# A hybrid encoder layer: the first norm applied behind the up projection, six accumulators through up and down, and waits moved in the first round, the first SSD group, the last norms and the tail

## The chip, the cores and the metric

The kernel runs on one core of one Trainium2 chip, as one launch. The metric is the device time of the launch in microseconds. Names of engines: TensorE (PE in the rows, PEld its weight loads), VectorE (DVE), ScalarE (ACT), GpSimd (POOL), and SyncE (SP), whose queue issues the weight loads.

## What is computed

One inference step of one layer, for 256 prompt frames and 32 sample frames together (T = 288 columns), all in fp32:

```python
proj = x @ w_in                                  # gates | z | xBC | dt | q_a | kv_a
y_ssm = SSD(causal_conv(xBC), dt) ... @ w_ssm_proj   # 8 groups of 4 heads, grouped RMSNorm
y_mla = attention(latent q, latent kv) @ w_mla_proj  # 16 heads, in 4 rounds of 4
mix = (sigmoid(g_ssm) * y_ssm + sigmoid(g_mla) * y_mla) @ w_out
h = LN1(ALPHA * x + mix)                         # over 1024 features, gain ln1_g, offset ln1_b
y = LN2(ALPHA * h + relu(h @ w_up)**2 @ w_down)  # w_up 1024 x 4096, w_down 4096 x 1024
```

Further outputs are the new latents, the rotated keys, the SSD states and the last conv rows.

## The kernel before

**Layout.** Features lie on the partitions, frames on the columns. Every dense weight comes in chunks of 128 x 1024 floats (512 KB), 204 loads in the order of `chunk_order()`: q and kv latents, four conv blocks (x0 to x3), four attention rounds with seven conv blocks each, eight SSD groups with two z blocks, two gate blocks and two chunks of the MLA projection (m), the SSM projection (s), the output projection (8 chunks, o), the up projection (32, u), the down projection (32, d).

**Splits.** A chunk passes a ring of five slots. SP loads it when the slot is free, ScalarE writes its high part (`hi`, L868), VectorE the rest (`lo`, L1242), and TensorE multiplies in three passes (`passes`, L406 to L408: high x high, high x low, low x high), 24 matmuls of 288 columns per chunk. On ScalarE and VectorE `ahead(name)` splits the chunk three places behind the named one, so the order of `ahead` calls among the other work is each engine's programme, written out by hand. Engines run in order: a wait blocks what stands behind it.

**Accumulators.** Dense results go to two banks of ps_acc in turns (`open_turn` waits for the evacuation of the block two turns earlier); four banks (ps_row, ps_cb, ps_tr, together ps_att) hold attention, SSD and the first half of s; ps_s and ps_ss hold sums and small products.

**Start and round 0.** GpSimd begins with four loads of the rotated key cache, kall. Later it copies conv edges (`conv`, L1764 and L1766), builds kab and kall from krot (L1777, L1779), then loads side, the latent caches and side_v. ScalarE evacuates each conv block (`conv_in`), VectorE adds three taps (`conv`, L1291), ScalarE applies silu (`conv_out_block`, L938). TensorE takes transposes of dt, acum and wend (L467) before dense x3.

**First SSD group.** VectorE and ScalarE finish conv block 31 before `decay_log(0)` (L1462 to L1472) and the exponentials. TensorE's `tokens(g, t)` (L676) waits for seg_sub and for btok (tr_free). In group 0 ScalarE and VectorE also split o (`o_high`, `o_low`, four calls of 1152 columns each).

**Last norms.** `spread(j, bank)` (L730) broadcasts a group's inverse deviation, `normed` (L1537) multiplies by it, and `norm_high` and `norm_low` split the result. Spreads 6 and 7 stand behind chunk s(0,0).

**First norm.** VectorE adds ax (ALPHA x) and each output block into d1 (`block_sum`, L1666), from block 4 on less a provisional mean. GpSimd adds blocks and squares (L1864), TensorE sums over the partitions with the ones matrix (`first_sum` L812, `last_sums` L816 to L821), VectorE makes mean and variance, ScalarE the root, VectorE the reciprocal (L1690), GpSimd subtracts the mean from six blocks (L1899). Then for each block: scale on VectorE (L1696), add the offset into h_h on ScalarE (L1198), h_l on VectorE (L1700). The first two up chunks wait for each h_lo.

**Up and down.** For an up block ScalarE takes the relu out of PSUM (L1209), VectorE squares (L1730), ScalarE writes ff_h, VectorE ff_l (L1722). Down sums 32 matmul groups per output block; the second norm goes as the first, and its output leaves in four transfers.

## Time and profile before

| | |
|---|---|
| median of 3 runs | 882.57 us (881.86 to 884.1) |
| profiled execution | 882.47 us |
| its span, first to last instruction | 880.7 us |
| mean granted TensorE clock | 0.987 |
| busy in the span | PE 95%, VectorE 62%, ScalarE 51%, GpSimd 11% |
| moved by DMA | 123.57 MB, 140 GB/s on average |

A row of waits names the waiting instruction, what released it, and the time in total, the number of times and the longest. A timeline row gives start, duration and instruction; a pause before it and its releaser stand in brackets; several instructions in a row are one entry with xcount. A group of instructions gives count, busy time, mean ns, and the idle time before them. A TensorE matmul's listed duration is modelled and overlaps its neighbours; the distance from start to start is what it costs. In a window row the busy times stand in the order PE, PEld, DVE, ACT, POOL.

### The profile page before, as it was taken

To read this page: it belongs to the slowest core of one execution; us is meant where nothing else is said; L and a number is where in the kernel's file an instruction comes from. 1 tells how busy PE (TensorE), PEld (TensorE's weight loads), DVE (VectorE), ACT (ScalarE), POOL (GpSimd) and SP (SyncE) were. 2 spreads that over 40 slices of the span, in tenths; PEclk is the share of its full clock that TensorE was granted. 3 is DMA by queue.
4 is the path that set the end of the run, shared out by engine and by line. 5 is a ranking of instruction groups with operands and counts; after the bars stand their busy time and mean duration, and the time that the engine had idled before them with its cause. 6 is when DMAs were issued, how large, how long until landed. Compare 5 with 4: busy or idle time off the path is not lost.

```text
span 880.7 us, 15552 instructions
## 1 busy us (share of the span) xinstructions
PE 833.2 (95%) x6363; PEld 789.3 (90%) x6363; DVE 550.2 (62%) x899; ACT 447.2 (51%) x745; POOL 95.1 (11%) x163
## 2 busy tenths in 40 slices
PE   5989999999999998899999999999859999999994
PEld 5978999999899998789999999899859999999994
DVE  4786646646646655877677677666477666644454
ACT  4684655555556557553555544453336555533332
POOL 1052010011101011000000000000160000000033
PEclk9999999999999999999999999999999999999997
DMA  8457335325325224344344334555423555555441
GB/s 305 124 167 266 97 98 168 120 95 169 102 91 174 88 70 142 102 130 135 125 133 131 126 128 120 186 167 168 134 82 125 167 165 167 167 168 168 145 143 54
DMA packets 34183, 123.57 MB, mean 140 GB/s; under 512 B 4224, under 2 KB 4368, under 8 KB 33856
## 3 DMA queue, kind: packets, MB, share of 16 engines
q1 hardware_dynamic: 30816, 110.67, 39.6%
q0 software_dynamic: 3104, 11.24, 3.7%
q8 instruction: 51, 0.84, 0.4%
q10 hardware_dynamic: 192, 0.66, 0.2%
q14 instruction: 20, 0.16, 0.1%
HBM read 118.52 MB, written 4.04 MB: 139 GB/s over the span
## 4 chain that ended last, share of the span: by engine, by line
PE 76%; DVE 8%; ACT 6%; DMA 4%; issue 3%; POOL 2%; SPq 0%; ACTq 0%; DVEq 0%; POOLq 0%
PE ps_acc L406 19%; PE ps_acc L408 19%; PE ps_acc L407 18%; DMA wraw<-in_wst 3%; PE ps_s L590 3%; ACT whi L868 2%; ACT prob L987 2%; DMA side_v<-in_ukT 1%; DVE wlo L1242 1%; PE ps_acc L503 1%; PE ps_row L704 1%; DVE prob L1403 1%; PE ps_ss L602 1%; PE ps_acc L505 1%; PE ps_acc L504 1%
## 5 line engine op out<-in xcount | busy, mean ns | idle before, releaser
L1242 DVE TENSOR_TENSOR wlo<-wraw,whi 128x1024 fp32r<-128x1024 f32 x204 | 250.4, 1229 | 214.9 <-ACT whi L868 214.1
L868 ACT CAST whi<-wraw 128x1024 fp32r<-128x1024 f32 x204 | 213.3, 1046 | 124.5 <-DMA wraw<-in_wst 124.2
L406 PE MATMUL ps_acc<-xh,whi 128*128 128x288 f32 x576 | 178.4, 310 | 9.3 <-DVE wlo L1242 8.6
L408 PE MATMUL ps_acc<-xh,wlo 128*128 128x288 f32 x576 | 170.9, 297 | 0.0
L407 PE MATMUL ps_acc<-xl,whi 128*128 128x288 f32 x576 | 169.0, 293 | 0.0
L406 PEld LDWEIGHTS ps_acc<-xh,whi 128*128 128x128 f32 x576 | 108.9, 189 | 16.6 <-DVE wlo L1242 8.9
L407 PEld LDWEIGHTS ps_acc<-xl,whi 128*128 128x128 f32 x576 | 109.9, 191 | 0.6
L408 PEld LDWEIGHTS ps_acc<-xh,wlo 128*128 128x128 f32 x576 | 108.7, 189 | 0.0
L406 PE MATMUL ps_acc<-h_h,whi 128*128 128x288 f32 x256 | 76.7, 299 | 6.4 <-DVE h_l L1700 6.3
L408 PE MATMUL ps_acc<-h_h,wlo 128*128 128x288 f32 x256 | 76.6, 299 | 0.0
L408 PE MATMUL ps_acc<-ff_h,wlo 128*128 128x288 f32 x256 | 75.9, 296 | 0.0
L406 PE MATMUL ps_acc<-ff_h,whi 128*128 128x288 f32 x256 | 75.9, 296 | 0.0
L407 PE MATMUL ps_acc<-h_l,whi 128*128 128x288 f32 x256 | 75.4, 295 | 0.0
L407 PE MATMUL ps_acc<-ff_l,whi 128*128 128x288 f32 x256 | 74.6, 292 | 0.0
L1291 DVE SCALAR_TENSOR_TENSOR cv<-xp,vec,cv 128x292 f32<-128x292 f32 x96 | 50.4, 525 | 10.8 <-ACT cv L933 8.3
L406 PEld LDWEIGHTS ps_acc<-h_h,whi 128*128 128x128 f32 x256 | 48.9, 191 | 7.1 <-issue 6.7
L407 PEld LDWEIGHTS ps_acc<-h_l,whi 128*128 128x128 f32 x256 | 49.5, 193 | 0.0
L407 PEld LDWEIGHTS ps_acc<-ff_l,whi 128*128 128x128 f32 x256 | 48.8, 191 | 0.1
L408 PEld LDWEIGHTS ps_acc<-h_h,wlo 128*128 128x128 f32 x256 | 48.7, 190 | 0.0
L406 PEld LDWEIGHTS ps_acc<-ff_h,whi 128*128 128x128 f32 x256 | 48.1, 188 | 0.1
L408 PEld LDWEIGHTS ps_acc<-ff_h,wlo 128*128 128x128 f32 x256 | 48.0, 187 | 0.0
L1766 POOL COPY cnew<-xp 128x6 f32<-128x6 f32 x32 | 14.8, 462 | 241.3 <-ACT xp L930 241.3
(356 smaller groups left out, 1818.9 us busy)
## 6 DMA issues: line engine op xcount, KB each, us to landing
wraw<-in_wst SPq DMA_DIRECT2D x204, 512.0 KB, 3.5
side<-in_ukT POOLq DMA_DIRECT2D x8, 256.0 KB, 3.8
side_v<-in_ukT POOLq DMA_DIRECT2D x8, 256.0 KB, 3.1
out_ssm<-s_out POOLq DMA_DIRECT2D x8, 256.0 KB, 2.5
x<-in_xT SPq DMA_DIRECT2D x2, 576.0 KB, 6.0
ax<-in_xT POOLq DMA_DIRECT2D x1, 1152.0 KB, 6.6
out_y<-d SPq DMA_DIRECT2D x4, 288.0 KB, 2.1
ckvT<-in_cacheT POOLq DMA_DIRECT2D x1, 1024.0 KB, 7.7
```

The costliest lines, as they stand in the source:

```text
L406: pe.matmul(out, w, mh, start=first, stop=False)
L407: pe.matmul(out, w, ml, start=False, stop=False)
L408: return pe.matmul(out, wl, mh, start=False, stop=last)
L503: pe.matmul(acc, ckv_h[:, k, f], hi, start=k == 0, stop=False)
L504: pe.matmul(acc, ckv_h[:, k, f], lo, start=False, stop=False)
L505: mm = pe.matmul(acc, ckv_l[:, k, f], hi, start=False, stop=k == RB - 1)
L590: mm = pe.matmul(ps_s[:, c * P:(c + 1) * P], ckvK[0:n, j, c * P:(c + 1) * P], ssT[0:n, j, :], start=j == 0, stop=j == 4)
L868: act.copy(whi[:, s % RING, :], wraw[:, s % RING, :]).then_inc(split_hi, 1)
L987: e = act.activation(prob[:, h4, a:b], prob[:, h4, a:b], ACT.Exp, bias=stat[:, 1, 4 * q + h4:4 * q + h4 + 1], accum_out=stat[:, 2, 4 * q + ...
L1242: tt(wlo[:, s % RING, :], wraw[:, s % RING, :], whi[:, s % RING, :].bitcast(F32), ALU.subtract).then_inc(split_lo, 1)
L1291: stt(cv[:, u, :], xp[:, u, 1 + tap:1 + tap + CW], v1(V_CONVW + tap * CB + b), cv[:, u, :], ALU.mult, ALU.add).then_inc(tap_chain if tap < ...
L1766: pool.tensor_copy(cnew[:, b, :].rearrange("p (a c) -> p a c", a=2), xp[:, u, 8:XW].rearrange("p (a c) -> p a c", c=36)[:, 6:8, 33:36]).th ...
```

## The change

**First norm.** The sum over x of the 8 blocks is made in round 0 (three adds on VectorE, one sum over ones on TensorE), and ScalarE makes cm = -ALPHA/1024 of it in round 1. ax becomes ALPHA x + cm, on VectorE (before: ALPHA x on ScalarE). For each output block, d1 is evacuated, ScalarE writes e_h = gamma d1 and the square, VectorE e_l. The up projection multiplies e, extended by two columns (gamma and the offset), so 290 columns instead of 288. Mean and inverse deviation come from reductions on VectorE and two sums over ones behind up(2). They are applied to the product: VectorE adds -mean times the gamma column and multiplies by the inverse deviation, ScalarE adds the offset column in the relu, squares, and casts. h itself is made in the down stage (`residual`).

**Accumulators.** Up and down use six banks in turn. `behind(b)` sets how far the evacuation lags: three to one blocks.

**Second norm.** The provisional mean is block 0's alone (first_sum behind d(1,1)); the running sums on TensorE stand ahead of d(7,3); squares are taken block by block; VectorE subtracts the mean from blocks 0 to 3 (before 0 and 1), GpSimd from 4 to 7 (before 2 to 7).

**Moves.** The kall loads go behind the kab copies on GpSimd, side_v's ahead of the cache loads; dense x3 ahead of the transposes; silu of block 2 behind the evacuation of qab; conv 31 behind decay_log(0); the o splits of VectorE into group 1 (ScalarE's into groups 0 and 1); norm_rows(0) behind start_state(4); spreads 6 and 7 behind s(1,0); norm_high(4) and normed(4), normed(5) ahead of a weight split; mix_low(6), mixed(7) and mix_low(7) ahead of one.

The diff, cut:

```diff
+UB = 6
+
+
+def behind(b):
+
+    return max(0, b - 3 + (b >= 12) + (b >= 20))
+
+
...
     dense(("x", 1), open_turn(("x", 1)))
     dense(("x", 2), open_turn(("x", 2)))
+    dense(("x", 3), open_turn(("x", 3)))
     pe.wait_ge(m_act, 6)
...
-    dense(("x", 3), open_turn(("x", 3)))
...
         pe.wait_ge(qnat_cp, i + 1)
         if i:
             pe.wait_ge(os_evac, i)
+            pe.wait_ge(cm_done, 1)
...
+        if i == 0:
+            pe.wait_ge(cm_red, 3)
+            pe.wait_ge(os_evac, 1)
+            pe.matmul(ps_ss[:, 0:T], ones, cm[:], start=True, stop=True).then_inc(cm_pe, 1)
...
         dense(("s", b, 0), ps_att[b], yn_rows, 0, True, False)
-        if b == 0:
+        if b == 1:
...
+    def first_sum():
+
+        pe.wait_ge(d_evac, 1)
+        pe.matmul(ps_s[:, 0:T], ones, d2[:, 0, :], start=True, stop=True).then_inc(ln_pe, 1)
+
+    def run_sums():
+
+        pe.wait_ge(ln_run, 10)
+        pe.matmul(ps_s[:, 0:T], ones, lnt[:, 1, 1, :], start=True, stop=False)
+        pe.wait_ge(ln_run, 11)
+        pe.matmul(ps_ss[:, 0:T], ones, lnt[:, 1, 2, :], start=True, stop=False)
+
+    def last_sums():
+        pe.wait_ge(d_evac, 8)
+        pe.matmul(ps_s[:, 0:T], ones, d2[:, 7, :], start=False, stop=True).then_inc(ln_pe, 1)
+        pe.wait_ge(ln_sq, 8)
+        pe.matmul(ps_ss[:, 0:T], ones, sq2[:, 7, :], start=False, stop=True).then_inc(ln_pe, 1)
...
-        if b == 4:
-            first_sum(0)
-    last_sums(0, d1)
...
+    def up(b):
+
+
         wait_split(("u", b))
-    out = [open_turn(("u", b)) for b in range(2)]
-    for k in range(KB):
-        pe.wait_ge(h_lo, k + 1)
-        for b in range(2):
-            mm = passes(out[b][:, 0:T], *part(("u", b), k), h_h[:, k, :], h_l[:, k, :], k == 0, k == 7)
-            if k == 7:
-                mm.then_inc(chunk_used, 1)
-    for b in range(2, FB):
-        dense(("u", b), open_turn(("u", b)), lambda k: (h_h[:, k, :], h_l[:, k, :]))
...
+        if b >= UB:
+            pe.wait_ge(u_evac, b - UB + 1)
+        elif b >= 4:
+            wait_evac(pe, ("o", 6))
+            wait_evac(pe, ("o", 7))
+        out = up_banks[b % UB]
+        for k in range(KB):
+            if b == 0:
+                pe.wait_ge(e_lo, k + 1)
+            mm = passes(out[:, 0:E], *part(("u", b), k), e_h[:, k, :], e_l[:, k, :], k == 0, k == 7)
+        mm.then_inc(chunk_used, 1)
+
+    pe.wait_ge(gb_lo, 2)
+    for b in range(FB):
+        up(b)
+        if b == 2:
+            for j, bank in enumerate((ps_s, ps_ss)):
+                pe.wait_ge(ln1_red, 3 * j + 3)
+                pe.matmul(bank[:, 0:T], ones, lnt[:, 0, 1 + j, :], start=True, stop=True).then_inc(ln1_pe, 1)
...
-        out = open_turn(("d", b, 0))
+        pe.wait_ge(u_evac, min(FB, FB + b - UB + 1))
+        if b >= UB:
+            pe.wait_ge(d_evac, b - UB + 1)
         for k in range(4):
-            dense(("d", b, k), out, ff_rows, 8 * k, k == 0, k == 3)
-            if b == 4 and k == 0:
-                first_sum(1)
-    last_sums(1, d2)
+            if b == KB - 1 and k == 3:
+                run_sums()
+            dense(("d", b, k), down_banks[b], ff_rows, 8 * k, k == 0, k == 3)
+            if b == 1 and k == 1:
+                first_sum()
+    last_sums()
...
-    conv_out_block(2)
...
         q_copy(i, 2, qab, 0)
+        if i == 0:
+            conv_out_block(2)
...
+        if i == 1:
+            act.wait_ge(cm_pe, 1)
+            act.activation(cm[:], ps_ss[:, 0:T], ACT.Identity, scale=-ALPHA / D_MODEL).then_inc(cm_done, 1)
...
+        act.wait_ge(cm_red, 3)
...
-    conv_out_block(CB - 1)
     wait_used(act, att_last)
-    act.wait_ge(conv_done, CB)
...
+        if g == 0:
+            conv_out_block(CB - 1)
...
+        if g == 1:
             o_high(2)
...
+        if g < 2:
+            o_high(3 * g)
...
+        if g == 0:
+            o_high(1)
...
+    mix_high(KB - 1)
     ahead(("o", 0))
-    mix_high(KB - 1)
...
+    def sum_square(b):
+        act.activation(sq1[:, b, :], d1[:, b, :], ACT.Square).then_inc(ln1_sq, 1)
+
+    def e_high(b):
+        wait_evac(act, ("o", b))
+        act.activation(e_h[:, b, 0:T], d1[:, b, :], ACT.Identity, scale=v1(V_LN1G + b)).then_inc(e_hi, 1)
...
+            act.copy(e_h[:, :, T:T + 1], v1(V_LN1G, KB).unsqueeze(2)).then_inc(gb_hi, 1)
+            act.copy(e_h[:, :, T + 1:E], v1(V_LN1B, KB).unsqueeze(2)).then_inc(gb_hi, 1)
+        if b >= 2:
+            e_high(b - 2)
+            sum_square(b - 2)
+    for b in range(KB - 2, KB):
+        e_high(b)
+        sum_square(b)
...
+    def activate(b):
+
+        act.wait_ge(u_step, 2 * b + 2)
+        act.copy(wb[:, b % 2:b % 2 + 1], up_banks[b % UB][:, T + 1:E]).then_inc(u_evac, 1)
+        act.wait_ge(u_evac, b + 1)
+        act.activation(rl[:, b % 2, :], rl[:, b % 2, :], ACT.Relu, bias=wb[:, b % 2:b % 2 + 1]
+                       ).then_inc(ff_step, 1)
+        act.wait_ge(ff_step, 2 * b + 1)
+        if b >= 2:
+            act.wait_ge(ff_lo, b - 1)
+        act.activation(ff[:, b % 2, :], rl[:, b % 2, :], ACT.Square).then_inc(ff_step, 1)
+        act.wait_ge(ff_step, 2 * b + 2)
         act.copy(ff_h[:, b, :], ff[:, b % 2, :]).then_inc(ff_hi, 1)
...
+        if b == 3:
+            act.wait_ge(ln1_step, 3)
+            act.activation(lnt[:, 0, 4, :], lnt[:, 0, 4, :], ACT.Sqrt, bias=v1(V_LNEPS)).then_inc(ln1_std, 1)
+        for u in range(behind(b - 1), behind(b)):
+            activate(u)
...
+        if i == 0:
+            dve.wait_ge(misc_done, 1)
+            tt(x0[:, 0:4, :], x0[:, 0:4, :], x0[:, 4:8, :], ALU.add).then_inc(cm_red, 1)
...
+    wait_used(dve, att_last)
+    decay_log(0)
     conv(CB - 1)
-    wait_used(dve, att_last)
-    dve.wait_ge(silu_done, CB)
-    decay_log(0)
...
+        if g == 1:
+            o_low(0)
...
+        if g == 1:
+            o_low(1)
...
+        if g == 1:
+            o_low(2)
+        elif g == 4:
+            norm_rows(0)
...
+    dve.wait_ge(ax_in, 16)
+    dve.wait_ge(cm_done, 1)
+    stt(ax[:], ax[:], ALPHA, cm[:].unsqueeze(1).to_broadcast([P, KB, T]), ALU.mult, ALU.add).then_inc(ax_done, 1)
...
+    mix_low(KB - 2)
+    mixed(KB - 1)
+    mix_low(KB - 1)
     ahead(("o", 0))
-    mixed(KB - 1)
-    mix_low(KB - 2)
-    mix_low(KB - 1)
...
+    def out_sum(b):
+        wait_used(dve, ("o", b))
+        tt(d1[:, b, :], ax[:, b, :], acc_of(("o", b))[:, 0:T], ALU.add).then_inc(acc_sem(("o", b)), 1)
+
+    def e_low(b):
+        dve.wait_ge(e_hi, b + 1)
+        stt(e_l[:, b, 0:T], d1[:, b, :], v1(V_LN1G + b), e_h[:, b, 0:T].bitcast(F32), ALU.mult,
+            ALU.subtract).then_inc(e_lo, 1)
...
+        out_sum(b - 1)
+        if b >= 2:
+            e_low(b - 2)
+    out_sum(KB - 1)
+    e_low(KB - 2)
+    e_low(KB - 1)
...
+    def scaled(b):
+
+        wait_used(dve, ("u", b))
+        if b >= 2:
+            dve.wait_ge(ff_step, 2 * b - 2)
+        acc = up_banks[b % UB]
+        stt(ff_t[:, b % 2, :], lnt[:, 0, 3, :], acc[:, T:T + 1], acc[:, 0:T], ALU.mult, ALU.add
+            ).then_inc(u_step, 1)
+        dve.wait_ge(u_step, 2 * b + 1)
+        tt(rl[:, b % 2, :], ff_t[:, b % 2, :], lnt[:, 0, 5, :], ALU.mult).then_inc(u_step, 1)
...
+        tt(tmp[:, 0:4, :], src[:, 0:4, :], src[:, 4:8, :], ALU.add).then_inc(ln1_red, 1)
+        dve.wait_ge(ln1_red, first + 1)
+        tt(tmp[:, 0:2, :], tmp[:, 0:2, :], tmp[:, 2:4, :], ALU.add).then_inc(ln1_red, 1)
+        dve.wait_ge(ln1_red, first + 2)
+        tt(out, tmp[:, 0, :], tmp[:, 1, :], ALU.add).then_inc(ln1_red, 1)
...
+        for u in range(behind(b - 1), behind(b)):
+            scaled(u)
+            if u:
+                ff_low(u - 1)
+        ahead(("u", b))
+        if b == 0:
+            block_sums(d1, lns, lnt[:, 0, 1, :], 0)
+            dve.wait_ge(ln1_sq, KB)
+            block_sums(sq1, sq1, lnt[:, 0, 2, :], 3)
+        if b == 2:
...
+            dve.wait_ge(ln1_std, 1)
+            dve.reciprocal(lnt[:, 0, 5, :], lnt[:, 0, 4, :]).then_inc(ln1_step, 1)
+            dve.wait_ge(ln1_step, 4)
+    for u in range(behind(FB - 1), FB):
+        scaled(u)
+        ff_low(u - 1)
+    ff_low(FB - 1)
...
+            tt(lxb[:, b % 2, :], d1[:, b, :], lnt[:, 1, 0, :], ALU.subtract).then_inc(ln_xb, 1)
+            dve.wait_ge(ln_xb, b)
+        wait_used(dve, ("d", b, 3))
+        tt(d2[:, b, :], lxb[:, b % 2, :] if b else d1[:, b, :], down_banks[b][:, 0:T], ALU.add
+           ).then_inc(d_evac, 1)
...
+    def residual(b):
+        tt(d1[:, b, :], d1[:, b, :], lnt[:, 0, 3, :], ALU.add).then_inc(ah_step, 1)
+        dve.wait_ge(ah_step, 2 * b + 1)
+        stt(d1[:, b, :], d1[:, b, :], v1(V_LN1G + b), lnt[:, 0, 5, :], ALU.mult, ALU.mult).then_inc(ah_step, 1)
...
+    dve.wait_ge(ln_sq, 8)
+    tt(d2[:, 0:4, :], d2[:, 0:4, :], lnt[:, 1, 3, :].unsqueeze(1).to_broadcast([P, 4, T]), ALU.add
+       ).then_inc(ln_w0, 1)
+    inverse()
+    dve.wait_ge(ln_w0, 1)
     for b in range(KB):
-        scaled(1, d2, b, V_LN2G)
+        if b >= 4:
+            dve.wait_ge(ln_w, b - 3)
+        stt(d2[:, b, :], d2[:, b, :], v1(V_LN2G + b), lnt[:, 1, 5, :], ALU.mult, ALU.mult).then_inc(ln_z, 1)
...
-    for q in range(4):
-        pool.dma_start(kall[32 * q:32 * q + 32, :, 0:PAST], kpeT.rearrange("(a p) k -> p a k", a=2)
-                       ).then_inc(kall_in, 16)
...
+    for q in range(4):
+        pool.dma_start(kall[32 * q:32 * q + 32, :, 0:PAST], kpeT.rearrange("(a p) k -> p a k", a=2)
+                       ).then_inc(kall_in, 16)
...
+    side_v_load(0)
     pool.dma_start(ckvT[:, :, 0:PAST], cacheT).then_inc(cache_in, 16)
     pool.dma_start(ckvK[:, 0:4, :], cacheK).then_inc(cache_in, 16)
-    side_v_load(0)
...
+    for b in range(4, KB):
+        pool.tensor_tensor(d2[:, b, :], d2[:, b, :], lnt[:, 1, 3, :], ALU.add).then_inc(ln_w, 1)
```

## Rows read from the trace of the kernel before

**Rows 1.** The page's engine totals: busy us (share of the span) xinstructions.

```profile
PE 833.2 (95%) x6363; PEld 789.3 (90%) x6363; DVE 550.2 (62%) x899; ACT 447.2 (51%) x745; POOL 95.1 (11%) x163
```

**Rows 2.** Waits of TensorE, whole span: waited-for: us in total, times, longest us.

```profile
PE ps_acc L406 <- DVE h_l L1700: 6.3, 1, 6.3
PE ps_tr L676 <- DVE btok L1481: 3.0, 2, 2.4
PE ps_tr L676 <- DVE segs L1469: 2.9, 2, 2.4
PE ps_acc L406 <- ACT qab L971: 2.4, 1, 2.4
...
PE ps_acc L406 <- DVE d L1666: 2.0, 2, 1.3
...
PE ps_acc L406 <- DVE mix_l L1635: 1.6, 1, 1.6
PE ps_s L730 <- DVE yt L1537: 1.6, 1, 1.6
PE ps_tr L467 <- DVE dend L1341: 1.4, 1, 1.4
...
PE ps_s L516 <- DMA side_v<-in_ukT: 1.2, 1, 1.2
```

**Rows 3.** Windows: us, busy us (xrecords) by engine, granted clock, DMA share, GB/s.

```profile
66.00:70.00 4.00, 4.00 (x20) 4.00 (x20) 3.93 (x7) 1.75 (x3) 2.71 (x5) 0.57 0.78 251
...
620.00:626.00 6.00, 5.25 (x26) 5.09 (x27) 2.83 (x6) 1.71 (x3) 0.00 (x0) 0.72 0.31 87
...
664.00:760.00 96.00, 95.90 (x725) 95.66 (x724) 63.21 (x93) 55.05 (x99) 0.00 (x0) 1.00 0.53 165
```

**Rows 4.** DMA queues, first 12 us: packets, MB, share of 16 engines.

```profile
q0 software_dynamic: 192, 0.52, 16.7%
```

**Rows 5.** Timelines of GpSimd and ScalarE: start us, us, operation, [idle before].

```profile
1.33 2.32 POOL L1753 DMA_DIRECT2D kall<-in_kpeT  x4 [0.88 <-POOLq L2002]
...
53.56 0.63 ACT L933 ACTIVATE cv<-xp,vec 128x292 f32<-128x292 f32 x1 [1.41 <-POOL xp L1764]
```

**Rows 6.** Timelines of TensorE and VectorE before the first SSD group.

```profile
337.53 0.22 PE L666 MATMUL ps_tr<-rows_s,ones_r 64*128 64x128 f32 x1
...
340.44 2.16 DVE L1462 SCALAR_TENSOR_TENSOR seg<-ps_row,tokv,con 128x128 f32<-128x128 f32 x8 [0.57 <-ACT xc L938]
```

**Rows 7.** TensorE timeline: first output, first down and last down matmul.

```profile
616.59 0.30 PE L406 MATMUL ps_acc<-mix_h,whi 128*128 128x288 f32 x1
...
763.35 0.29 PE L406 MATMUL ps_acc<-ff_h,whi 128*128 128x288 f32 x1
...
867.03 0.30 PE L408 MATMUL ps_acc<-ff_h,wlo 128*128 128x288 f32 x1
```

**Rows 8.** Groups by form, 664 to 762 us: xcount, busy us, mean ns, idle before.

```profile
L1242 DVE TENSOR_TENSOR wlo<-wraw,whi 128x1024 fp32r<-128x1024 f32 x31 | 38.0, 1226 | 16.2 <-ACT whi L868 16.1
L1730 DVE TENSOR_TENSOR ff<-rl 128x288 f32<-128x288 f32 x31 | 14.2, 458 | 17.1 <-ACT rl L1209 17.1
...
L868 ACT CAST whi<-wraw 128x1024 fp32r<-128x1024 f32 x32 | 33.6, 1051 | 0.9 <-DMA wraw<-in_wst 0.9
...
L1209 ACT ACTIVATE rl<-ps_acc 128x288 f32<-128x288 f32 x31 | 12.7, 411 | 40.2 <-PE ps_acc L408 40.2
L1215 ACT ACTIVATE d<-d,lnb 128x288 f32<-128x288 f32 x8 | 4.3, 538 | 0.0
```

**Rows 9.** Timelines of VectorE and GpSimd in the tail.

```profile
872.93 4.64 DVE L1696 SCALAR_TENSOR_TENSOR d<-d,vec,lnt 128x288 f32<-128x288 f32 x8
...
869.36 5.76 POOL L1899 TENSOR_TENSOR d<-d,lnt 128x288 f32<-128x288 f32 x6 [9.42 <-DVE lnt L1680]
```

**Rows 10.** ScalarE's last table load and the activation behind it, timeline.

```profile
556.80 1.28 ACT L1096 ACT_TABLE_LOAD   x1
558.09 0.54 ACT L1096 ACTIVATE rstd<-rstd,vec 128x288 f32<-128x288 f32 x1
```

297 lines of the change are left out of this document (114 added, 183 removed).

## The prediction

> **What bounds the kernel now.** I read the engine totals first: TensorE is busy 95% of the span and VectorE 62% [rows 1]. The matmul stream is therefore the bound, and a change that leaves its work alone can win only TensorE's pauses and the stretches at the half clock. The waits of TensorE list those pauses with their releasers [rows 2]; the windows tell where the granted clock was not full: 0.57 at 66 to 70 us, behind the 2.4 us pause for qab, and 0.72 at 620 to 626 us, behind the 1.6 us pause for mix_l. Between 664 and 760 us it was 1.00, with 725 matmul records in 96.00 us, so 0.1324 us from matmul to matmul [rows 3]. That is the unit for everything below. The profiled execution took 882.47 us (span 880.7 and 1.8 around it), 0.1 us under the median of 882.57, so the sum needs no correction.
>
> **Start.** GpSimd's four loads of kall leave the beginning. In the first 12 us their queue holds 16.7% of the time of the 16 DMA engines [rows 4], 2.0 us for all of them, just when x and the first weights queue behind. Everything that lands after them can come up to 2.0 us earlier, the first matmul somewhat less, since part of kall's packets fall behind the first weights. I take 1.6 us; bounds 0.5 and 2.0. **Sum: -1.6.**
>
> **Round 0.** Three moves. (a) dense x3 goes ahead of the transposes that wait 1.4 us for dend. (b) ScalarE's silu of block 2 goes behind the evacuation of qab, for which TensorE waits 2.4 us. (c) side_v is issued ahead of the two 1 MB cache loads, so the 1.2 us wait for it goes [rows 2]. But the kall loads come back here: the four issues took 2.32 us and now stand between the kab copies and GpSimd's copy for conv block 1, and ScalarE is already waiting 1.41 us for that copy [rows 5]. So ScalarE, and VectorE behind it, start block 1 some 2.3 us later; behind them stand the evacuations of x2 and x3 that the two halves of the q projection need. Walking the queues on (estimates): TensorE reaches q at about 58.4 us instead of 59.9, waits there for x2 (until 60.7), x3 (until 63.9) and the first q half, and comes to the k projection at about the old time. (a) and (b) are given back, (c) stays. The half clock there may stay or go; it costs 1.3 us, for the window 66 to 70 holds 20 records where 30 would fit [rows 3]. I take -0.9; bounds: the three waits (5.0) and the clock all won, -6.3; and the kall issues paid in full with no gain but (c), +1.1. The estimate sits nearer the upper end because the row of the copy shows ScalarE waiting on exactly the queue that is lengthened. **Sum: -0.9.**
>
> **The new sum over x (cm).** VectorE adds three operations of 1152, 576 and 288 elements, about 2.6 us (estimated from 1.23 us for 1024 and 0.46 for 288 [rows 8]), behind the split of the v weights, where VectorE next waits for a weight load; without that cover they would cost 2.6. TensorE adds one sum over the ones matrix, 0.6 us with its change of operands, in its stream. ScalarE's activation in round 1 and the two new waits (cm_red, cm_done) have a round of time. **Sum: +0.6.**
>
> **First SSD group.** VectorE begins decay_log(0) only at 340.44 us, behind the last conv block and its silu, though its rows are there at 337.75 [rows 6]; TensorE waits 2.4 us of the 2.9 for segs, and then 2.4 of the 3.0 for btok [rows 2], which VectorE writes late because ScalarE put two conversions of o ahead of a weight split. With decay_log first, it ends 2.6 us earlier and the first wait closes (-2.4). The conv block now runs behind it, so the second wait only falls to about 1.3 us (-1.1). The 0.5 us wait of group 1 goes too (-0.5), since three o_low operations (1152 elements, 1.35 us each by the same estimate) no longer stand ahead of decay_log(1). All four now stand in group 1, 4.0 us more than before on VectorE, in holes that hold all but 0.4 us (+0.4); o_lo is what the m projection waits for. Bounds -4.3 and -2.5. **Sum: -3.6.** Moving norm_rows(0) in group 4 is worth nothing: ScalarE's three table loads set that pause, and the reciprocal runs beside them.
>
> **Last norms.** The spreads 6 and 7 go behind s(1,0), 3.2 us later; yt, awaited 1.6 us [rows 2], is then ready. **Sum: -1.6.** The scaling of ax on VectorE (2304 elements, about 2.6 us) delays weight splits that are two chunks ahead, under 6.4 us of matmuls; without them it would cost its 2.6.
>
> **From the first output matmul to the first down matmul.** Now 616.59 to 763.35, 146.8 us [rows 7]. It contains the pauses for mix_l, for d, the 6.3 us before h_l [rows 2], five sums over ones and the half clock of [rows 3]. After the change nothing there waits for the norm: weights multiply d1*gamma directly, and mean and deviation are applied to the product behind the up projection. What is left is 960 matmuls x 0.1324 = 127.1, two sums of 0.6 = 1.2, and two more columns in 768 matmuls. Those are not in the trace; by the unit above a column costs at most 0.1324 / 288 = 0.46 ns, so 0.7 us in all (bounds 0 and, for a row length that no longer suits, twice that). Total 129.0. Who is late next? e_low(7) comes about 1.7 us after the last output matmul (three steps of about 0.5 and their semaphores), and up(0) needs it after 21 matmuls, 2.8 us; the six accumulators let up run to block 5, some 19 us, before the first evacuation is due, and the inverse deviation is there after about 16 (six reductions, a sum behind up(2), four steps and three splits on VectorE). **Sum: -17.8.**
>
> **Does the work behind each up block fit into 24 matmuls (3.18 us)?** VectorE: split 1.15 plus three of 0.46 = 2.5. ScalarE: split 1.05, relu with a pointer bias 0.54, square and cast 0.41 each, and a one-column copy, under the 0.41 of 288 columns and taken at 0.2 = 2.6 [rows 8], in a chain of own semaphores. I take it as covered, with 0.5 us left per block and two blocks of lead.
>
> **Down stage.** Now 103.7 us [rows 7]; 767 steps are 101.6, three sums 1.8, none of them late (first_sum stands behind d(1,1), its operand by then 2 us old). **Sum: -0.3.**
>
> **Tail.** Two sums leave it and the last two start earlier (-0.4); the subtraction on VectorE is twice as wide (+0.6); GpSimd has four instead of six of 0.96, and VectorE's eight scalings, 4.64 us or 0.58 each beside it [rows 9] against 0.46 for such an operation alone [rows 8], have the port to themselves (-0.7 of the 0.9, as ScalarE's additions follow behind). One of GpSimd's 0.96 us steps can stand in the way of the wide subtraction, which takes back up to 1.0. Bounds -1.2 and +0.8. By the Trainium skill, "SBUF — State Buffer", on the shared port, an operation of VectorE with two SBUF inputs and one of GpSimd that reads SBUF exclude each other, whichever began first; the trace agrees (0.58 against 0.46 each), and by the rule alone the change would win the whole 0.9 there. **Sum: -0.5.**
>
> **Total**: -1.6 -0.9 +0.6 -3.6 -1.6 -17.8 -0.3 -0.5 = -25.7; 882.5 - 25.7 = **856.8 us**.
>
> **Rivals.**
> 1. *Round 0 costs more*: the kall issues are slowed by VectorE's work, and the q projection starts later. Three us over the forecast: 859.8. Speaks for it: the 1.41 us wait; against: an issue is short, 0.58 us each in the row [rows 5], so a doubling is needed. Chance 0.15.
> 2. *The evacuation chain sets the pace of up*: five dependent steps with 0.15 us of semaphore more each make 3.4 us per block, 0.25 x 32 = +8: 864.8. Against it: ScalarE waits 40.2 us for TensorE in this stage today [rows 8]. Chance 0.08.
> 3. *Slower than before*: table loads. If square, relu and sqrt did not share a table, each up block would hold two loads of 1.28 us, the next activation 1.29 us after its load's start [rows 10]. ScalarE then needs 5.2 us, 2.0 over the matmuls, 32 x 2.0 = +65: 921. It decides from 4.0 us per block on, where 0.8 x 32 eats the 25.7. Against it: no load follows 558 us, though relu and square do. Chance 0.03. By the Trainium skill, "ScalarE: Activation LUTs", What ACT_TABLE_LOAD costs, a switch is a load of 1.28 us and a drain of 1.38, 2.66 us; this would be +150 us. The trace has no such drain behind the load.
> 4. *More*: round 0 keeps (a) and (b) and its clock, and the first group closes both waits: -5: 851.8. Chance 0.10.
> 5. *It does not do what it says*: the mean or the deviation comes too late and TensorE stands at up block 6 as long as it stood before h_l: +6.3 and the clock: 864.6. Chance 0.02.
>
> The forecast has 0.62. The range 850 to 865 holds it and all but the third. A measurement of this kernel tells 0.3%, 2.6 us, from no change; all but the third lie far beyond that: faster 0.95, same 0.02, slower 0.03.
>
> **What the profile after would show.** First matmul about 1 us earlier; conv block 1's cv still waiting for GpSimd, longer than 1.41; no pause at h_l, yt, mix_l; no window under full clock after 600 us; first up matmul within 0.2 us of the last output matmul; 3.2 us per up block; the span from the first output to the first down matmul 129 us; the tail from the last down matmul 13 instead of 13.5 us. The prediction is wrong if TensorE's waits after 660 us name rl, ff_l or wlo, or if round 0 ends later than now.

## The result and the profile after

The changed kernel takes **857.69 us** (median of 4 runs, 857.42 to 859.12) against 882.35 us for the kernel before in the same job (4 runs, 881.86 to 884.1). The ratio is 0.9716, with a 95% interval of 0.9695 to 0.9738: 24.7 us less. The prediction was 856.8 us, range 850 to 865. The profiled execution has a span of 855.7 us at a mean granted clock of 0.994, against 880.7 and 0.987.

The totals and the clock row of the page (40 slices, tenths), to be held against [rows 1]:

```profile
PE 828.9 (97%) x6359; PEld 787.1 (92%) x6359; DVE 568.5 (66%) x947; ACT 471.3 (55%) x817; POOL 79.7 (9%) x144
...
PEclk9999999999999999999999999999999999999998
```

TensorE is busy 97% instead of 95%; VectorE and ScalarE took over what the norm and its accumulators cost and have 18 and 24 us more work. What fell is TensorE's waiting. Its waits over the whole span (waited-for: us in total, times, longest), against [rows 2]:

```profile
PE ps_acc L426 <- DVE wlo L1300: 8.3, 1, 8.3
PE ps_acc L426 <- ACT xp L970: 2.4, 1, 2.4
PE ps_tr L701 <- DVE btok L1546: 1.7, 3, 0.6
PE ps_acc L426 <- ACT qn L1010: 1.2, 1, 1.2
PE ps_row L594 <- DVE prob L1461: 0.8, 4, 0.2
PE ps_s L848 <- DVE d L1809: 0.6, 1, 0.6
PE ps_ss L545 <- DVE ssc L1427: 0.6, 1, 0.6
```

The names h_l, segs, qab, mix_l, yt, dend and side_v are gone, and so is a wait of 0.6 us for xl at the start (more on it below); xp, qn and ssc are new, and all three stand in round 0. The first line is the wait for the first weights. The stages, from TensorE's timeline (start us, duration, instruction), against [rows 7]: first output matmul, first up matmul, first and last down matmul.

```profile
609.09 0.30 PE L426 MATMUL ps_acc<-mix_h,whi 128*128 128x288 f32 x1
...
635.28 0.29 PE L426 MATMUL ps_row<-e_h,whi 128*128 128x290 f32 x1
...
739.72 0.29 PE L426 MATMUL ps_cb<-ff_h,whi 128*128 128x288 f32 x1
...
842.60 0.29 PE L428 MATMUL ps_tr<-ff_h,wlo 128*128 128x288 f32 x1
```

The last output matmul starts at 635.15, the first up matmul 0.13 us behind it: there is no pause where TensorE stood 6.3 us before. From the first output to the first down matmul it is now 130.6 us instead of 146.8. Two windows (us, busy us and records by engine, clock, DMA share, GB/s) answer to [rows 3]: the half clock behind mix_l is gone, and the up stage runs at the full clock, with both helpers busier than before.

```profile
620.00:626.00 6.00, 6.00 (x48) 6.00 (x47) 4.04 (x6) 2.78 (x6) 0.00 (x0) 1.00 0.54 172
...
646.00:738.00 92.00, 92.00 (x685) 92.00 (x684) 74.91 (x123) 73.14 (x148) 0.00 (x0) 1.00 0.51 162
```

### The profile page after: what moved, and what is told of

The parts are those of the page before. It is cut to its first block, busy times and chain, and to the rows that moved or that the text cites. A ratio compares the mean times of both kernels' runs of the same rounds, so it can differ in the third digit from the quotient of the medians.

```text
span 855.7 us, 15623 instructions
## 1 busy us (share of the span) xinstructions
PE 828.9 (97%) x6359; PEld 787.1 (92%) x6359; DVE 568.5 (66%) x947; ACT 471.3 (55%) x817; POOL 79.7 (9%) x144
## 4 chain that ended last, share of the span: by engine, by line
PE 83%; ACT 6%; DVE 6%; DMA 2%; issue 1%; POOL 1%; ACTq 0%; DVEq 0%; POOLq 0%
PE ps_acc L426 15%; PE ps_acc L428 14%; PE ps_acc L427 14%; PE ps_row L428 3%; PE ps_row L426 3%; PE ps_row L427 3%; PE ps_s L611 3%; PE ps_cb L428 2%; PE ps_tr L428 2%; PE ps_tr L426 2%; PE ps_cb L426 2%; PE ps_tr L427 2%; PE ps_cb L427 2%; ACT prob L1026 2%; DVE wlo L1300 1%; DMA wraw<-in_wst 1%
## 5 line engine op out<-in xcount | busy, mean ns | idle before, releaser
L426 PE MATMUL ps_acc<-o_h,whi 128*128 128x288 f32 x128 | 39.9, 311 | 0.0
L428 PE MATMUL ps_acc<-o_h,wlo 128*128 128x288 f32 x128 | 37.9, 296 | 0.0
L427 PE MATMUL ps_acc<-o_l,whi 128*128 128x288 f32 x128 | 37.4, 293 | 0.0
L426 PE MATMUL ps_acc<-q_h,whi 128*128 128x288 f32 x96 | 29.7, 310 | 3.8 <-ACT xp L970 2.4
L428 PE MATMUL ps_acc<-q_h,wlo 128*128 128x288 f32 x96 | 29.0, 302 | 0.0
L427 PE MATMUL ps_acc<-q_l,whi 128*128 128x288 f32 x96 | 28.6, 298 | 0.0
L428 PE MATMUL ps_row<-e_h,wlo 128*128 128x290 f32 x96 | 28.6, 298 | 0.0
L426 PE MATMUL ps_row<-e_h,whi 128*128 128x290 f32 x96 | 28.6, 297 | 0.0
L427 PE MATMUL ps_row<-e_l,whi 128*128 128x290 f32 x96 | 28.5, 297 | 0.0
L427 PEld LDWEIGHTS ps_acc<-o_l,whi 128*128 128x128 f32 x128 | 24.3, 190 | 0.3
```

Source lines behind the costliest of these rows:

```text
L426: pe.matmul(out, w, mh, start=first, stop=False)
L427: pe.matmul(out, w, ml, start=False, stop=False)
L428: return pe.matmul(out, wl, mh, start=False, stop=last)
```

## Experiments

Each kernel is the changed one with the edit shown. The following table gives, for all profiled executions, the starts of the sum over misc (TensorE's 49th matmul), the first q matmul, the first output, first up, first down and last down matmul, and the end of the span (us, from the timelines). It is read by differences: the first column varies from run to run for reasons of its own, told below, and everything behind it is carried along.

| kernel | misc | q | output | up | down | last down | span |
|---|---|---|---|---|---|---|---|
| before | 17.57 | 59.89 | 616.59 | 659.63 | 763.35 | 867.03 | 880.7 |
| changed | 16.28 | 59.73 | 609.09 | 635.28 | 739.72 | 842.60 | 855.7 |
| kall_first | 17.16 | 58.04 | 607.63 | 633.67 | 738.10 | 840.99 | 854.1 |
| kall_mid | 17.47 | 58.34 | 608.34 | 634.52 | 738.96 | 841.85 | 854.9 |
| kall_ssc_rows | 17.36 | 58.19 | 606.79 | 632.97 | 737.60 | 840.47 | 853.6 |
| cols_288 | 17.12 | 60.56 | 609.90 | 636.01 | 740.22 | 843.11 | 856.2 |
| cols_296 | 16.75 | 60.21 | 609.68 | 635.68 | 741.40 | 844.29 | 857.4 |
| four_acc | 16.15 | 59.59 | 609.34 | 635.70 | 752.91 | 855.79 | 868.9 |
| act_double | 16.79 | 60.24 | 610.31 | 636.51 | 747.46 | 851.53 | 864.6 |
| up_tables | 17.45 | 60.93 | 612.00 | 638.10 | 800.30 | 920.96 | 934.0 |
| conv_first | 16.07 | 59.51 | 612.29 | 638.34 | 742.77 | 845.66 | 858.7 |
| o_splits_back | 16.28 | 59.71 | 611.63 | 637.87 | 742.31 | 845.19 | 858.3 |
| spreads_back | 17.05 | 60.48 | 612.08 | 638.35 | 742.79 | 845.67 | 858.7 |
| tail_split | 16.84 | 60.28 | 610.09 | 636.32 | 740.75 | 843.63 | 857.2 |

### The kall loads in round 0: kall_first and kall_mid

The theory on record: the four loads, put ahead of GpSimd's conv copies, give back what (a) and (b) win. The rows of the changed kernel, timelines of GpSimd, ScalarE and TensorE:

```profile
52.21 2.31 POOL L1891 DMA_DIRECT2D kall<-in_kpeT  x4 [0.30 <-POOL kab L1888]
...
54.85 0.63 ACT L973 ACTIVATE cv<-xp,vec 128x292 f32<-128x292 f32 x1 [3.99 <-POOL xp L1873]
...
59.73 0.58 PE L426 MATMUL ps_acc<-q_h,whi 128*128 128x288 f32 x1 [2.44 <-ACT xp L970]
```

The issues end, the copy follows, ScalarE starts, and TensorE waits 2.44 us for the evacuation behind it.

kall_first puts the loads back at GpSimd's beginning:

```diff
+            for q in range(4):
+                pool.dma_start(kall[...], kpeT...).then_inc(kall_in, 16)
             conv(0)
...
             pool.wait_ge(kab_done, 8)
-            for q in range(4):
-                pool.dma_start(kall[...], kpeT...).then_inc(kall_in, 16)
             for b in range(1, X_FIRST):
                 conv(b)
```

> The changed kernel with one part undone: GpSimd's four loads of kall stand at the beginning again. Theory A (the prediction's): the start loses what it had won, 1.3 us (first matmul of the input projection back near 8.6 us); the copy for conv block 1, for which ScalarE waits 3.99 us at 54.85, comes 2.3 us earlier, the wait falls to about 1.6, and with it TensorE's pause of 2.44 us before the q projection goes. The later places win at least 1.1 us more than the start loses: about 856.6 us. Theory B: the copy isn't what the q projection waits for (the weight loads and VectorE's order are), the pause stays above 1.5 us, and only the loss at the start is left: 859.0 us.

kall_mid puts them behind the conv copies, not ahead of them:

```diff
             pool.wait_ge(kab_done, 8)
-            for q in range(4):
-                pool.dma_start(kall[...], kpeT...).then_inc(kall_in, 16)
             for b in range(1, X_FIRST):
                 conv(b)
+            for q in range(4):
+                pool.dma_start(kall[...], kpeT...).then_inc(kall_in, 16)
```

> The changed kernel with the four kall loads put behind GpSimd's copies for conv blocks 1 to 3 (issued at about 63 us instead of 52 us), where the DMA engines are nearly idle (share 0.02 between 60 and 65 us). kall is first read at 93 us. Theory A: ScalarE's wait of 3.99 us for the copy falls to about 1.6, the pause of 2.44 us before q goes, the start keeps its 1.3 us, and round 0 passes on 2.0 to 2.4 us: about 855.5 us. Theory B: the weight loads between 70 and 80 us (DMA share 1.00) land no earlier, so what is won before q comes back as a longer pause behind the ssc copy at 83.5 us (0.58 us now): 857.2 us or more.

Measured: kall_first 856.98 us, ratio 0.9707 (0.9672 to 0.9742); kall_mid 856.39 us, 0.9692 (0.9664 to 0.9721). The totals alone don't separate them from the changed kernel; the places do. Timelines of ScalarE and TensorE, then the window of the q projection, in kall_mid:

```profile
53.46 0.63 ACT L973 ACTIVATE cv<-xp,vec 128x292 f32<-128x292 f32 x1 [1.41 <-POOL xp L1873]
...
61.43 0.40 PE L426 MATMUL ps_acc<-q_h,whi 128*128 128x288 f32 x1 [1.25 <-ACT xp L970]
```

ScalarE's wait is 1.41 us, as before the change, and from the sum over misc to q it is 40.87 us in kall_mid and 40.88 in kall_first against 43.45 in the changed kernel: 2.6 us, as theory A has it. TensorE's pause of 2.44 us in front of q is gone. In the changed kernel the half clock stood behind it (0.51 between 60 and 63 us); here the clock is at 1.00 there, and a pause of 1.25 us for the next evacuation takes its place, so that the first chunk of q lasts 5.07 us in both. Then 0.2 us (kall_first) to 0.6 us (kall_mid) come back in front of the transposes of ssc (pause 0.78 and 1.21 us instead of 0.58), which is theory B's mechanism at a third of its price. At the first output matmul 1.9 us of the 2.6 are left in kall_mid and 2.3 in kall_first, counted from misc.

### The start

kall_first was to lose 1.3 us at the beginning, with its first matmul back near 8.6 us. That matmul starts at 8.44 us, those of the twelve profiles without kall at the start between 8.18 and 8.42, the one before at 8.61. What the loads of kall delay is the second half of x. Timelines of ScalarE and TensorE, the changed kernel, then kall_first, then the kernel before:

```profile
7.28 1.15 ACT L916 CAST xh<-x 128x1152 fp32r<-128x1152 f32 x1 [0.41 <-DMA x<-in_xT]
```

```profile
9.35 1.15 ACT L916 CAST xh<-x 128x1152 fp32r<-128x1152 f32 x1 [2.23 <-DMA x<-in_xT]
...
11.95 0.61 PE L426 MATMUL ps_acc<-xh,whi 128*128 128x288 f32 x1 [0.27 <-DVE xl L1310]
```

```profile
9.77 1.16 ACT L876 CAST xh<-x 128x1152 fp32r<-128x1152 f32 x1 [2.48 <-DMA x<-in_xT]
...
12.37 0.40 PE L406 MATMUL ps_acc<-xh,whi 128*128 128x288 f32 x1 [0.63 <-DVE xl L1252]
```

In the twelve profiles without kall that conversion starts between 7.17 and 7.68 us. So the loads behind kall do land some 2 us later, as the prediction took it. But TensorE is still at work on the first half of x at that time, and it pays a pause of only 0.27 us in kall_first and 0.63 us before; none of the twelve has one.

The rest of this stretch varies by chance. Windows 12 to 16 us of the changed kernel and of kall_mid:

```profile
12.00:16.00 4.00, 4.00 (x32) 4.00 (x31) 1.37 (x2) 2.15 (x4) 0.18 (x1) 1.00 1.01 379
```

```profile
12.00:16.00 4.00, 4.00 (x23) 4.00 (x23) 1.34 (x2) 2.20 (x4) 0.19 (x1) 1.00 0.85 308
```

Both kernels do the same there, yet one shows 32 matmul records and the other 23. In the timelines the matmuls are 0.24 us apart until 11.6 us in the one and until 14.2 us in the other, then 0.13. Over the twelve profiles that end lies between 11.1 and 14.2 us, and the later it is, the later misc starts (11.06 with 16.07, 12.67 with 16.75, 14.19 with 17.47). It is the moment at which TensorE leaves its half clock, and it costs up to 1.4 us by chance. The granted clock of these windows reads 1.00 all the same, so here the spacing tells it, not the clock column.

What is kall's share? The changed kernel has 13 steps of 0.24 us, kall_first and the kernel before have 12, so the half clock was nearly the same in these three. From the first matmul to misc they take 8.00, 8.73 and 8.96 us. With the later first matmul (0.15 and 0.32 us) that makes 0.9 us for kall_first and 1.3 us for the kernel before, which is the whole difference of the two first profiles. Held against profiles of the twelve whose half clock ended at the same moment, it is 0.4 and 0.8 us. Whether the pause itself shortens the stretch at the half clock no run shows, so the share stays between these values.

### What two more columns cost: cols_288, cols_296

```diff
-                    mm = passes(out[:, 0:E], ..., e_h[:, k, :], e_l[:, k, :], ...)
+                    mm = passes(out[:, 0:T], ..., e_h[:, k, 0:T], e_l[:, k, 0:T], ...)
```

(ScalarE and VectorE then read columns 287 and 286 in place of the two extra ones.)

> The changed kernel with the two extra columns (gamma and offset) left out of the up projection's matmuls: 288 columns instead of 290; mean and offset are then taken from two ordinary columns, so the first norm is not applied rightly, while every other instruction stays. Theory A (the prediction's term): a column costs 0.46 ns, the up stage gets 0.7 us shorter. Theory B (read from the profile of the changed kernel, 0.1344 us from matmul to matmul there against 0.1324 before): 290 columns cost 2.0 ns more than 288, the stage gets 1.5 us shorter. Theory C: the pace comes from something else behind the up projection (the evacuations), and it stays at 0.1344.

```diff
-E = T + 2
+E = T + 8
```

(The offset's column fills the six new ones.)

> The changed kernel with 296 instead of 290 columns in the up projection's matmuls (the offset's column repeated six times more; the result is the same). Theory A: 0.46 ns a column: 2.7 ns for each of 768 matmuls, 2.1 us more. Theory B: the step comes in larger units (beyond 288 a group of columns is charged whole), so 296 costs what 290 does: 0 us. Theory C: a fixed price of about 1 ns for a row length that isn't a multiple of something and 0.46 ns a column: below 2.1 us, about 1.3.

Measured: 857.85 us (0.9711, 0.9668 to 0.9754) and 859.39 us (0.9728, 0.9685 to 0.9772). The up stage (first up to first down matmul) takes 104.44 us with 290 columns, 104.21 with 288 and 105.72 with 296. Taking both columns away again gives back 0.23 us, not 0.7 and not 1.5. But 288 columns cost less elsewhere: from bank to bank in the timelines, a chunk of 24 matmuls takes 3.173 us in the down stage, 3.226 in cols_288, 3.233 in the changed kernel and 3.273 in cols_296. So theory C holds for cols_288 as far as the pace goes, but not for its reason: cols_296 shows that the columns do set the pace, and below, act_double keeps 3.23 us per chunk while ScalarE is busy nearly all the time. The kernel before settles one more point: its up stage multiplied 288 columns out of rows 288 apart (h_h, h_l) at 3.173 us per chunk. So it is not the stage that costs. What cols_288 leaves as it was is where the rows begin: e_h and e_l are 290 elements per row.

### Rows, kall and ssc in one kernel: kall_ssc_rows

```diff
+ES = T + 8
...
-        e_h = after("e_h", [P, KB, E], F32R)
-        e_l = after("e_l", [P, KB, E], F32R)
+        e_h = after("e_h", [P, KB, ES], F32R)
+        e_l = after("e_l", [P, KB, ES], F32R)
...
-                    mm = passes(out[:, 0:E], ..., e_h[:, k, :], e_l[:, k, :], ...)
+                    mm = passes(out[:, 0:E], ..., e_h[:, k, 0:E], e_l[:, k, 0:E], ...)
...
                 ahead(("k", i, 0))
-                ahead(("k", i, 1))
-                qnat_copy(i)
+                if i:
+                    ahead(("k", i, 1))
+                qnat_copy(i)
+                if i == 0:
+                    ahead(("k", i, 1))
```

and the edit of kall_mid.

> The changed kernel with three further edits at three places, each read in its own stretch. (1) kall's loads behind the conv copies as in the run kall_mid. (2) In round 0 VectorE copies ssc ahead of a weight split that waits for a load under full DMA engines. (3) The rows of e_h and e_l lie 296 elements apart instead of 290; the matmuls still read 290 columns. Theory A for (3): not the columns but where a row begins in memory costs (288 columns out of rows 290 apart took 0.1340 us a matmul, before they took 0.1324 and less); the up stage goes from 104.44 to 103.2 us. Theory B for (3): 290 columns cost 0.1343 us wherever the row begins: 104.4. Theory A for (2): TensorE's pause before the transposes of ssc, 1.21 us in kall_mid, goes, and 0.7 to 1.2 us stay won; theory B: the next weight chunk is late by the same load, and nothing is won. Together: 854.4 us by the A's, 856.4 by the B's.

Measured: **855.01 us**, ratio 0.9681 (0.9667 to 0.9696), the fastest of all. Edit (3) is not the reason: the up stage takes 104.63 us, if anything 0.2 more (3.240 us per chunk). Theory A for the rows falls: rows that begin at multiples of 32 bytes don't bring 290 columns to the cost of 288. Edit (2) is, with (1): TensorE's transposes of ssc come without a pause, and from misc to the first output matmul it is 589.44 us against 590.87 in kall_mid and 592.81 in the changed kernel. VectorE's timeline, with the copy now ahead of the split that waits for a load:

```profile
78.10 0.69 DVE L1428 COPY ssc<-ps_s 128x512 f32<-128x512 f32 x1 [4.11 <-PE ps_s L537]
80.93 1.23 DVE L1301 TENSOR_TENSOR wlo<-wraw,whi 128x1024 fp32r<-128x1024 f32 x1 [2.14 <-ACT whi L909]
```

### Six accumulators: four_acc

```diff
-UB = 6
+UB = 4
...
-        up_banks = [*ps_att, ps_acc[:, 0, :], ps_acc[:, 1, :]]
+        up_banks = [*ps_att]
...
-                elif b >= 4:
-                    wait_evac(pe, ("o", 6))
-                    wait_evac(pe, ("o", 7))
```

> The changed kernel with four accumulators instead of six through the up and down stages (the four of ps_att). Theory A (the prediction's walk of who is late next): in the profile of the changed kernel up block 4 would begin at 649.4 us, while block 0's evacuation ends at 652.1 us, behind the reciprocal of 648.91. TensorE pauses 2.7 us there, the clock may fall behind it (up to 1.3 us), and with a lag of three blocks on four banks some 0.3 us of waits follow: about 3.0 to 4.5 us more than six banks, 861.5. Theory B: the evacuation catches up by itself and six banks buy nothing: 857.7. Theory C: without spare banks each block waits for its chain, 0.3 us for each of 28: 866.

Measured: 870.39 us (0.9866, 0.9837 to 0.9895); the up stage takes 117.21 us, 12.8 more. Timeline and window:

```profile
652.64 0.37 PE L426 MATMUL ps_row<-e_h,whi 128*128 128x290 f32 x1 [2.88 <-ACT wb L1239]
...
662.24 0.37 PE L426 MATMUL ps_cb<-e_h,whi 128*128 128x290 f32 x1 [1.38 <-ACT wb L1239]
...
688.16 0.37 PE L426 MATMUL ps_row<-e_h,whi 128*128 128x290 f32 x1 [2.29 <-ACT wb L1239]
```

```profile
648.00:660.00 12.00, 9.12 (x57) 8.91 (x56) 9.11 (x13) 5.57 (x11) 0.00 (x0) 0.86 0.27 85
```

The first pause is theory A's: 2.88 us where 2.7 were walked out, and 0.86 of the clock behind it. But four more follow (1.4 to 2.3 us); the last stands in front of block 12, and behind it there is none. At block 12 `behind` goes from three blocks of lag to two. With a lag of three on four banks, up(b) needs the evacuation of block b - 4, which ScalarE does only behind the split of chunk b + 3, whose load waits until block b - 2 has been multiplied. ScalarE's timeline ahead of the second pause shows this circle:

```profile
660.99 1.04 ACT L905 CAST whi<-wraw 128x1024 fp32r<-128x1024 f32 x1 [4.47 <-DMA wraw<-in_wst]
661.94 0.15 ACT L1239 COPY wb<-ps_cb 128x1 f32<-128x1 f32 x1
```

It waits 4.47 us for the load, splits, copies the offset column, and 0.3 us later TensorE goes on. So the fifth and sixth bank do two things, bridge the wait for the deviation and allow the lag. The five pauses make 9.8 of the 12.8 us, the four later ones 6.9; what lies between the expected 3.0 to 4.5 us and the 12.8 is mostly this second part. That a smaller lag on four banks would cure it is read from the place where the pauses end; no run of its own shows it.

### Room on ScalarE: act_double and up_tables

```diff
                     if s >= RING:
                         act.wait_ge(chunk_used, s - RING + 1)
+                    if SEQ_OF[("u", 5)] <= s <= SEQ_OF[("u", 31)]:
+                        act.copy(whi[:, s % RING, :], wraw[:, s % RING, :]).then_inc(m_act, 1)
+                        act.wait_ge(m_act, s - SEQ_OF[("u", 5)] + 7)
                     act.copy(whi[:, s % RING, :], wraw[:, s % RING, :]).then_inc(split_hi, 1)
```

> The changed kernel with one cost doubled: in the up stage ScalarE converts each weight chunk twice (27 chunks, 1.05 us each, one behind the other; the result is the same). Theory A (sum of busy time against matmuls): ScalarE has 2.62 us of work and 0.57 us of waits for loads behind each up block of 3.22 us; with 1.1 us more it needs 3.75, which is 0.5 us over the matmuls for 27 blocks, 13.7 us, less a lead of the splits of about 5 us: 9 us more, 866.5. Theory B (the evacuation chain sets the pace already, as in the prediction's second rival): every added microsecond shows, 27 x 1.1: 887. Theory C: the chain has so much slack that nothing shows below 4 us per block: 857.7.

Measured: 866.23 us (0.9819, 0.979 to 0.9847), 8.5 more, where the sum gave 9. In the window 660 to 700 us ScalarE is busy 38.54 of 40 us (32.67 in the changed kernel), and TensorE hardly notices; it begins to pause behind 698 us, when the lead of the splits is used up. The longest pause:

```profile
660.00:700.00 40.00, 39.89 (x296) 39.52 (x295) 27.98 (x46) 38.54 (x70) 0.00 (x0) 1.00 0.50 158
```

```profile
715.68 0.40 PE L426 MATMUL ps_acc<-e_h,whi 128*128 128x290 f32 x1 [2.04 <-DVE wlo L1303]
```

By the markers, 7.7 us of it lie in the up and the down stage. Where ScalarE is the bound, a block takes 3.60 us, against 3.75 in the sum. Theory A holds: the stage pays when the sum of busy time exceeds the matmuls, and the chain of dependent steps has no price beside it.

```diff
                 act.wait_ge(u_evac, b + 1)
+                act.activation(tb[:, 0:1], v1(V_LNEPS), ACT.Exp)
+                act.activation(tb[:, 1:2], v1(V_LNEPS), ACT.Sqrt)
                 act.activation(rl[:, b % 2, :], rl[:, b % 2, :], ACT.Relu, ...)
```

> The changed kernel with two table switches put into each evacuation of an up block: behind the copy of the offset column ScalarE does one exponential and one root of a single column, whose results nobody reads. This measures the price of the prediction's third rival. Theory A (load 1.28 us, next activation 1.29 us after the load's start, as in the profile before): 2.9 us more per block with the two small operations, ScalarE then needs 5.5 to 5.6 us against 3.22: 32 x 2.3 less 5 us of lead, 69 us more: 927. Theory B: by the Trainium skill, "ScalarE: Activation LUTs", What ACT_TABLE_LOAD costs, a switch also drains the engine for 1.38 us; then a block takes 8.3 us, 157 us more: 1015.

Measured: one run of 935.82 us, 78 us more than the changed kernel. ScalarE's timeline, one block:

```profile
692.04 1.04 ACT L909 CAST whi<-wraw 128x1024 fp32r<-128x1024 f32 x1
692.99 0.15 ACT L1243 COPY wb<-ps_row 128x1 f32<-128x1 f32 x1
693.16 1.28 ACT L1245 ACT_TABLE_LOAD   x1
694.45 0.20 ACT L1245 ACTIVATE tb<-vec 128x1 f32<-128x1 f32 x1
694.66 1.28 ACT L1246 ACT_TABLE_LOAD   x1
695.95 0.20 ACT L1246 ACTIVATE tb<-vec 128x1 f32<-128x1 f32 x1
696.06 0.52 ACT L1247 ACTIVATE rl<-rl,wb 128x288 f32<-128x288 f32 x1
696.61 0.44 ACT L1252 ACTIVATE ff<-rl 128x288 f32<-128x288 f32 x1
697.09 0.43 ACT L1254 CAST ff_h<-ff 128x288 fp32r<-128x288 f32 x1
697.43 1.04 ACT L909 CAST whi<-wraw 128x1024 fp32r<-128x1024 f32 x1
```

A block takes 5.39 us (692.04 to 697.43), 2.15 over the matmuls, and 32 of them make 69 us. By the markers the up stage takes 57.8 us more and the down stage, which begins with the splits behind, 17.8; the other 2.9 lie ahead of both, where the kernel is unchanged. Why the two stages make 75.6 and not 69 isn't split up; pauses of 6.69 and 10.8 us at 752 and 825 us stand where ScalarE evacuates two and three blocks one behind the other. Relu, square and cast need no load of their own behind the root. The next activation starts 1.29 us after its load (693.16, 694.45), and in all 64 loads of the stage the load takes 1.28 us. By the Trainium skill, "ScalarE: Activation LUTs", What ACT_TABLE_LOAD costs, each switch would take 2.66 us with a drain; an estimate from that page's figure makes a block 8.1 us and the kernel about 1015. The trace has no drain, and the measurement decides.

### The first SSD group: conv_first and o_splits_back

```diff
+            conv(CB - 1)
             wait_used(dve, att_last)
+            dve.wait_ge(silu_done, CB)
             decay_log(0)
-            conv(CB - 1)
...
+            conv_out_block(CB - 1)
             wait_used(act, att_last)
+            act.wait_ge(conv_done, CB)
...
-                if g == 0:
-                    conv_out_block(CB - 1)
```

> The changed kernel with one move of the first SSD group undone: conv block 31 and its silu stand ahead of decay_log(0) and the exponentials again; the splits of o stay where the change put them. Theory A: TensorE's first wait of that group comes back (+2.5 us), and the second one, 0.56 us now, goes, since block 31 no longer stands between: 2.0 us more, 859.7. Theory B: the first wait has another cause by now (the start of the sequence comes earlier than before), and it stays closed: 857.7. Theory C: both waits are the same delay passed on, and the second stays beside the first: 2.5 us or more, 860.3.

```diff
                 z_block(g, 0)
+                if g == 0:
+                    o_high(0)
+                    o_high(1)
                 ahead(("z", 2 * g + 1))
                 z_block(g, 1)
-                if g == 1:
+                if g == 0:
                     o_high(2)
...
-                if g < 2:
-                    o_high(3 * g)
+                if g == 0:
+                    o_high(3)
...
-                if g == 1:
-                    o_low(0)
...
-                if g == 1:
-                    o_low(1)
...
-                if g == 1:
+                if g == 0:
-                    o_low(2)
+                    o_low(0)
```

(o_low(1) and o_low(2) follow in group 0 in their old places, o_low(3) in group 1.)

> The changed kernel with the other half of the first SSD group undone: the four splits of o in group 0 again (ScalarE's conversions ahead of weight splits there), decay_log(0) still ahead of conv block 31. Theory A (the splits of o made the second wait): TensorE's wait for btok in group 0 goes from 0.56 to about 2.4 us, the 0.54 us in group 1 goes: 1.3 us more, 859.0. Theory B (conv block 31 and the delay of the first wait made it): it stays below 1 us, and the time at 857.3. With the run conv_first the two halves add up to the 4.7 us of the whole only by theory A.

Measured: conv_first 860.87 us (0.9758, 0.973 to 0.9787), o_splits_back 861.06 us (0.975, 0.9726 to 0.9774); from misc to the first output matmul 3.4 and 2.5 us more than the changed kernel. Pause and window in conv_first, and the pause in o_splits_back:

```profile
342.27 0.55 PE L701 MATMUL ps_tr<-con,xc 128*128 128x128 f32 x2 [2.36 <-DVE segs L1534]
```

```profile
343.00:347.00 4.00, 4.00 (x21) 3.53 (x20) 1.59 (x5) 3.83 (x5) 0.00 (x0) 0.65 0.06 22
```

```profile
350.95 0.28 PE L701 MATMUL ps_tr<-con,xc 128*32 128x128 f32 x1 [2.67 <-DVE btok L1547]
```

In conv_first the first wait is back at its old 2.36 us, the clock falls to 0.65 behind it (21 records in 4 us where the changed kernel has 33, some 1.5 us), and the second wait (0.56) is gone: 2.4 + 1.5 - 0.6 = 3.3. In the profile before, the same pause of 2.36 us had left the clock at 1.00. So theory A of conv_first has both waits right, and the clock, which none of the three theories had, adds 1.5 us. In o_splits_back the second wait is 2.67 us, and the 0.55 us for segs in group 1 is back: theory A again in its waits, at 2.5 us instead of 1.3. Its timelines of ScalarE and VectorE name the culprit:

```profile
343.91 2.20 ACT L1152 CAST o_h<-o 128x1152 fp32r<-128x1152 f32 x2
...
347.09 1.23 DVE L1301 TENSOR_TENSOR wlo<-wraw,whi 128x1024 fp32r<-128x1024 f32 x1 [3.30 <-ACT whi L908]
```

ScalarE's two conversions of o stand ahead of its weight split, VectorE waits 3.30 us for that split, and btok stands behind it. Without the clock's 1.5 us the two halves make 1.9 + 2.5 = 4.4 us, near the 4.6 us that the whole move won at this place.

### Last norms and tail: spreads_back and tail_split

```diff
-                if b == 1:
+                if b == 0:
                     pe.wait_ge(norm_t, 5)
...
-            normed(4, ps_ss)
-            norm_low(4)
-            normed(5, ps_s)
             ahead(("s", 0, 0))
+            normed(4, ps_ss)
+            norm_low(4)
+            normed(5, ps_s)
```

> The changed kernel with the last norms undone: the spreads 6 and 7 stand behind chunk s(0,0) again, and the norm steps of group 4 and 5 behind a weight split. Theory A (the prediction's): TensorE waits 1.6 us for yt again: 859.3 us, and no more, since nothing else in that stretch is late. Theory B: the wait is longer, or takes the clock down with it: 860.5. Theory C: the later start of the stretch has moved VectorE ahead, no wait: 857.7.

```diff
-            tt(d2[:, 0:4, :], d2[:, 0:4, :], lnt[:, 1, 3, :]...[P, 4, T], ALU.add)
+            tt(d2[:, 0:2, :], d2[:, 0:2, :], lnt[:, 1, 3, :]...[P, 2, T], ALU.add)
...
-                if b >= 4:
-                    dve.wait_ge(ln_w, b - 3)
+                if b >= 2:
+                    dve.wait_ge(ln_w, b - 1)
...
-            for b in range(4, KB):
+            for b in range(2, KB):
                 pool.tensor_tensor(d2[:, b, :], d2[:, b, :], lnt[:, 1, 3, :], ALU.add)
```

> The changed kernel with one part of the tail undone: VectorE subtracts the last mean from blocks 0 and 1 alone, GpSimd from 2 to 7 (six operations of 0.96 to 1.1 us). Theory A (the prediction's): the eight scalings on VectorE then run beside GpSimd at 0.58 us instead of 0.45 us each, +1.0 us, against 0.6 us that the narrower subtraction saves: the stretch from the last down matmul to the end grows from 13.1 to 13.5 us, 858.1 us. Theory B: the scalings keep 0.45 us, and the tail gets 0.6 us shorter: 857.1. Theory C: the last scaling waits for GpSimd's sixth block (at about 851.5 us): about 0.3 us more than A.

Measured: spreads_back 860.10 us (0.9739, 0.9717 to 0.9761), with 1.51 us of wait for yt, the clock at 1.00, and 2.2 us more from misc to the first output matmul, of which 1.9 lie behind round 0: theory A in mechanism, 0.3 us more in size. tail_split takes 858.84 us (0.9724, 0.9703 to 0.9746); from the last down matmul to the end it takes 13.55 us against 13.08. Scalings and GpSimd's additions, first in the changed kernel, then in tail_split:

```profile
844.84 4.43 POOL L1996 TENSOR_TENSOR d<-d,lnt 128x288 f32<-128x288 f32 x4 [8.65 <-DVE lnt L1821]
...
845.74 1.38 DVE L1853 TENSOR_TENSOR d<-d,lnt 128x1152 f32<-128x1152 f32 x1
...
849.02 3.57 DVE L1860 SCALAR_TENSOR_TENSOR d<-d,vec,lnt 128x288 f32<-128x288 f32 x8
```

```profile
845.87 5.76 POOL L1996 TENSOR_TENSOR d<-d,lnt 128x288 f32<-128x288 f32 x6 [8.65 <-DVE lnt L1821]
...
849.45 4.64 DVE L1860 SCALAR_TENSOR_TENSOR d<-d,vec,lnt 128x288 f32<-128x288 f32 x8
...
850.90 1.04 DVE L1860 SCALAR_TENSOR_TENSOR d<-d,vec,lnt 128x288 f32<-128x288 f32 x1
...
851.87 0.51 DVE L1860 SCALAR_TENSOR_TENSOR d<-d,vec,lnt 128x288 f32<-128x288 f32 x1
```

In tail_split the eight scalings take 4.64 us, in the changed kernel 3.57, so 1.07 saved against 0.60 for the wider subtraction (1.38 - 0.78). Theory A in its sum. But the 0.58 us per scaling is a mean that no scaling has: two of the eight, the second and the third, meet GpSimd's last two additions and take 1.04 us each; the later ones take 0.51, as in the changed kernel, where all but the first do. What is paid is about half a microsecond for each addition of GpSimd that a scaling meets, here twice.

## Why the prediction was right, and where not

The total was off by 0.9 us, but its terms were off by up to 1.7 with both signs: added up without signs the errors make 4.7 us, and that they leave 0.7 is luck. What isn't luck is the term that makes the change, which has its mechanism right and nine tenths of its size. Each term as the two first profiles show it, corrected by the runs (together 25.0 us, the difference of the spans):

- **Start, -1.6 forecast.** 1.3 measured between the two first profiles, of which the first matmul has 0.3 (about 1 was forecast for it). The loads land some 2 us earlier, as the prediction says. The step that failed handed nearly all of that delay on to TensorE, which had the first half of x to multiply meanwhile: kall_first pays 0.4 to 0.9 us for it. The sum is near because the kernel before paid more at this place (0.8 to 1.3 us) than kall_first; why, no run shows. And a term of this size is no larger than what chance does here.
- **Round 0, -0.9.** 0.2 measured. At the first x4 matmul the changed kernel is 2.3 us earlier than before, 1.0 of it won since misc, which is the forecast; behind the ssc copy and at dense x5 0.2 of that is left. The walk's mechanism is shown by kall_mid and kall_first: the kall issues gave (a) and (b) back, 2.6 us. The step that failed is a wait the walk left out, for ssc, whose copy stands behind a split that waits for its load.
- **cm, +0.6.** 0.4 measured. No row had the 0.6 us that the prediction takes for a sum over ones; the two sums in the up stage cost 1.0 us together.
- **First SSD group, -3.6.** 4.6 measured. The second wait was forecast at 1.3 us and is 0.56. The failed step charged conv block 31 to VectorE's path; but VectorE had 4.5 us of idle time a few operations behind decay_log(0) before (waiting for ScalarE's split) and has 1.2 now, and the block lies in it. o_splits_back shows that ScalarE's two conversions of o made that wait.
- **Last norms, -1.6.** 1.8 measured; spreads_back gives 1.5 us of wait.
- **First output to first down matmul, -17.8.** 16.1 measured. The mechanism holds at every point: no wait for h_l or d, no half clock, the evacuation chain late for nobody. The walk of who is late next holds too: the inverse deviation is there 15.6 us behind the first up matmul (about 16 forecast), and the first block that needs a used bank begins at 20.4 us. Two sizes were off. The output stage took 26.2 instead of 25.4 us, with two steps of 0.3 to 0.4 us at chunk boundaries in it. The up stage took 104.4 instead of the 103.6 that the terms make: the two columns and what comes with them cost 2.5 ns a matmul (3.233 against 3.173 us per 24), 1.9 us in all, where 0.7 was taken with an upper end of 1.5. The mis-sized term is that of the columns: cols_288 shows that they themselves cost 0.2 us and the rest is something else about these operands.
- **Down, -0.3.** 0.8 measured. The 103.7 us before held a pause in front of its sum over ones, which the prediction's sum had not named. It went, and two more sums stand in the stage now. TensorE's timeline before:

```profile
818.97 0.51 PE L812 MATMUL ps_s<-lnt,con 128*128 128x288 f32 x1 [1.51 <-POOL lnt L1864]
```

- **Tail, -0.5.** 0.57 measured, and tail_split confirms both signs. By the Trainium skill, "SBUF — State Buffer", Who interferes with whom, an operation of VectorE with two SBUF inputs contends with one of GpSimd that reads SBUF; the trace agrees, 1.04 us for a scaling that meets an addition of GpSimd and 0.51 for one that doesn't.

Of the rivals, the first (kall issues slowed by VectorE) is refuted by the row: 2.31 us for the four, 2.32 in [rows 5]. The second is refuted by act_double: with 1.1 us more per block ScalarE was still in time for ten chunks and more, and the whole cost 8.5 us, not 30. The 0.15 us that this rival took for each dependent step stands in no row; in up_tables such steps follow each other on ScalarE 0.02 to 0.04 us apart. The third has the price that the rows gave it, 2.15 us over the matmuls per block. Rival 4 had its second half right (the first group nearly closed both waits), and its first half exists as kall_mid and kall_ssc_rows. The fifth did not come; something like it is what four_acc does, at 12.8 us where the rival had 6.3.

**Open** is why a matmul of 288 columns costs 134.4 ns in cols_288 and 132.2 ns in the down stage, and in the up stage before. It is not the load of ScalarE, and for 290 columns not rows at multiples of 32 bytes. The two cheap cases read 288 columns out of rows 288 apart, so the distance of the rows, or the place of e in memory, is what is left; no run shows it. Rows at larger multiples weren't tried either, for there was no memory.

## What to carry to other kernels

When loads land late, ask what the engine has to do meanwhile: here a delay of 2 us cost TensorE between 0.4 and 1.3 us. When a step is moved on a queue, list who waits behind its new place: four DMA issues of 0.58 us on GpSimd cost TensorE 2.6 us, and behind the next two copies they cost nothing. Put a copy that TensorE waits for ahead of a weight split that may itself wait for a load. A spare accumulator is worth what the evacuation order makes of it: count the banks and the lag together, and charge a moved operation only if its engine has no idle time where it lands.

## What the runs showed of the hardware

- Kernels that are the same at their start leave the first half-clock stretch between 11.1 and 14.2 us, worth 1.4 us of the total. By the Trainium skill, "TensorE: Matmul & The Clock Gate", What you observe, that point varies from run to run by half a microsecond to either side; the spacing of the records here agrees that it varies, but over 3.1 us, and the measurement decides. Differences under 1.4 us are read from one marker to another, not from the totals: misc to q was 43.43 to 43.48 us in all nine further profiles that left this stretch alone.
- A pause of 2.36 us left the clock at 1.00 in one kernel and at 0.65 in another at the same place; 1.51 us for yt and 2.67 us for btok left it at 1.00, while before the change 1.6 us for mix_l had taken it to 0.72 [rows 3]. The length of a pause of this size doesn't tell its price: the chunk behind it is either as fast as ever or about 1.5 us longer.
- Columns aren't priced alone: 288, 290 and 296 columns out of the rows of e cost 134.4, 134.7 and 136.4 ns in the up stage, 288 out of rows 288 apart cost 132.2 in the down stage and in the up stage before. By the Trainium skill, "TensorE: Matmul & The Clock Gate", Back-to-back issue gap, a matmul at the full clock takes its columns at 2.4 GHz and 2.5 ns; an estimate from that makes two more columns 0.8 ns. The trace shows 0.3 from one side and 2.5 from the other.
- A scaling on VectorE that meets an addition on GpSimd takes 1.04 us instead of 0.51, and GpSimd's addition 1.00 instead of 0.79 (tail_split): both pay.
